# The forget-gate bias of eight attention heads: two matmuls against one-hot operands in place of one matmul against a prepared key tile

## The reference

```
log_f = jax.nn.log_sigmoid(f_logit + b_forget)          # 8 heads, 272 positions
cum = jnp.cumsum(log_f, axis=1).transpose(0, 2, 1)
s = (jnp.einsum('bhqd,bhkd->bhqk', q, k_f) * f_scale
     + c_q - cum[:, :, None, :])                        # c_q is cum at the query
p = jax.nn.softmax(jnp.where(mask, s, -jnp.inf), axis=-1)
o = jnp.einsum('bhqk,bhkd->bhqd', p, v_f)
```

## Time and profile before

| | |
|---|---|
| three runs | 2033.62, 2035.77 (the median), 2036.28 us |
| the profiled execution | 2033.62 us, of which the profile's span is 2031.8 us |
| PE busy | 1917.5 us, 94% of the span |
| DVE, ACT, POOL busy | 70%, 58%, 7% |
| matmul records | 10360, of them 96 of line 508 |

### The profile page before, as it was taken

The page is one execution under the profiler, slowest core; times in us unless marked ns, Lnnn a source line. Parts: engine busy times, 40 slices in busy tenths (PEclk is TensorE's granted clock), DMA queues, the critical chain, the costliest instruction groups (busy, mean ns, idle before and its releaser), DMA issues.

```text
span 2031.8 us, 28523 instructions
## 1 busy us (share of the span) xinstructions
PE 1917.5 (94%) x10360; PEld 1616.7 (80%) x10360; DVE 1432.1 (70%) x1529; ACT 1185.5 (58%) x1298; POOL 141.2 (7%) x184
## 2 busy tenths in 40 slices
PE   6999989999879999878999999999999999999997
PEld 5986789757868999867887887878878788788785
DVE  5542545435885555785887888888888788887885
ACT  4443453434634444634777667676776767767774
POOL 0102101120520000330000000000000000000000
PEclk9985799758888999987999999999999999999998
DMA  6420244103334546332798988989989899898892
GB/s 262 156 73 1 101 148 143 42 1 132 124 128 154 188 141 208 104 105 104 300 349 323 351 340 326 358 318 347 352 330 343 318 353 355 321 342 336 344 348 82
DMA packets 67847, 464.84 MB, mean 229 GB/s; under 512 B 7990, under 2 KB 8662, under 8 KB 15926
## 3 DMA queue, kind: packets, MB, share of 16 engines
q1 hardware_dynamic: 67061, 461.15, 60.7%
q0 software_dynamic: 704, 2.63, 0.4%
HBM read 462.71 MB, written 1.05 MB: 228 GB/s over the span
## 4 chain that ended last, share of the span: by engine, by line
PE 82%; DVE 8%; issue 7%; ACT 2%; DMA 0%; POOL 0%; ACTq 0%; SPq 0%; DVEq 0%; POOLq 0%
PE bank L356 22%; PE bank L357 22%; PE bank L358 22%; DVE wlo L347 2%; PE bank L506 2%; PE bank L793 2%; PE bank L801 2%; PE bank L443 2%; DVE cacc L1369 2%; DVE csq L1369 1%; PE bank L546 1%; PE bank L547 1%; PE bank L830 1%; PE bank L508 1%; ACT whi L342 1%
## 5 line engine op out<-in xcount | busy, mean ns | idle before, releaser
L347 DVE TENSOR_TENSOR wlo<-raw,whi 128x2048 fp32r<-128x2048 f32 (+2 forms) x454 | 1012.5, 2235 | 318.8 <-ACT whi L342 317.8
L342 ACT ACTIVATE whi<-raw 128x2048 fp32r<-128x2048 f32 (+2 forms) x454 | 844.7, 1863 | 278.9 <-PE bank L358 276.7
L356 PE MATMUL bank<-uhi,whi 128*128 128x272 f32 (+2 forms) x1200 | 355.2, 296 | 27.9 <-DVE ulo L1191 20.2
L356 PE MATMUL bank<-whi,hthi 128*128 128x512 f32 x896 | 366.9, 410 | 7.8 <-DVE wlo L347 7.8
L357 PE MATMUL bank<-wlo,hthi 128*128 128x512 f32 x896 | 356.2, 398 | 0.0
L358 PE MATMUL bank<-whi,htlo 128*128 128x512 f32 x896 | 356.0, 397 | 0.0
L358 PE MATMUL bank<-uhi,wlo 128*128 128x272 f32 (+2 forms) x1200 | 348.7, 291 | 0.0
L357 PE MATMUL bank<-ulo,whi 128*128 128x272 f32 (+2 forms) x1200 | 348.4, 290 | 0.0
L356 PEld LDWEIGHTS bank<-uhi,whi 128*128 128x128 f32 (+1 forms) x1200 | 232.0, 193 | 32.3 <-issue 22.8
L357 PEld LDWEIGHTS bank<-ulo,whi 128*128 128x128 f32 (+1 forms) x1200 | 232.0, 193 | 0.6
L358 PEld LDWEIGHTS bank<-uhi,wlo 128*128 128x128 f32 (+1 forms) x1200 | 231.6, 193 | 0.0
(11 more groups left out here) (276 smaller groups left out, 2256.1 us busy)
## 6 DMA issues: line engine op xcount, KB each, us to landing
raw<-in_wm SPq DMA_DIRECT2D x338, 1024.0 KB, 4.9
raw<-in_w SPq DMA_DIRECT2D x65, 1024.0 KB, 4.8
raw<-in_w SPq DMA_DIRECT2D x20, 768.0 KB, 4.1
raw<-in_w SPq DMA_DIRECT2D x16, 704.0 KB, 3.9
raw<-in_w SPq DMA_DIRECT2D x13, 512.0 KB, 3.6
raw<-in_w SPq DMA_DIRECT2D x2, 576.0 KB, 3.6
qk<-in_hT SPq DMA_DIRECT2D x1, 1088.0 KB, 9.1
gmb<-in_gmb POOLq DMA_DIRECT2D x1, 1024.0 KB, 6.7
```

What stands on the lines that cost most here:

```text
L342: act.activation(whi[:, n % RING, 0:c], raw[:, n % RAW, 0:c], ACT.Copy).then_inc(hi_ready, 1)
L347: dve.tensor_tensor(wlo[:, n % RING, 0:c], raw[:, n % RAW, 0:c], whi[:, n % RING, 0:c].bitcast(F32), ALU.subtract).then_inc(lo_ready, 1)
L356: pe.matmul(out, s_hi, m_hi, start=start, stop=False, skip_group_check=shared)
```

## The change

The 40-row matmul is replaced by two of 8 rows. The first has `ncum` as the stationary operand and, as the moving one, a one-hot column of the identity matrix, repeated over the keys with a step of zero. The second has the same column, repeated over the queries, as the stationary operand and `cum` as the moving one. `kcum`, `key_cum` and the semaphore `kcum_ready` go; PE waits for `cum_ready` instead. The copies go too, so that the logit tiles have 8 rows in place of 104, all at rows 0 to 7.

```diff
-FOX_AT = 32
-FOX_K = FOX_AT + FOX_HEADS
-FOX_ROWS = HEAD + FOX_K
-FOX_COPIES = (0, FOX_AT, HEAD, HEAD + FOX_AT)
...
-        cum = sb("cum", [FOX_ROWS, LEN], scope=first)
-        ncum = sb("ncum", [FOX_ROWS, LEN], scope=first)
-        kcum = sb("kcum", [FOX_ROWS, 2, LEN], scope=first)
+        cum = sb("cum", [FOX_HEADS, LEN], scope=first)
+        ncum = sb("ncum", [FOX_HEADS, LEN], scope=first)
...
-                    pe.wait_ge(kcum_ready, l * FOX_HEADS + (f + 1))
+                    pe.wait_ge(cum_ready, 2 * l + 2)
...
                     mm = pe.matmul(out, qk[part:part + HEAD, tq, q0:q0 + rows], qk[part:part + HEAD, tk, 0:keys], start=True, stop=not fox)
                     if fox:
-                        mm = pe.matmul(out, ncum[HEAD * (f % 2):HEAD * (f % 2) + FOX_K, q0:q0 + rows],
-                                       kcum[HEAD * (f % 2):HEAD * (f % 2) + FOX_K, (f // 2) % 2, 0:keys], start=False, stop=True)
+
+                        head = ident[0:FOX_HEADS, f:f + 1]
+                        pe.matmul(out, ncum[:, q0:q0 + rows], head.to_broadcast([FOX_HEADS, keys]), start=False, stop=False)
+                        mm = pe.matmul(out, head.to_broadcast([FOX_HEADS, rows]), cum[:, 0:keys], start=False, stop=True)
...
-            for at in (FOX_AT, HEAD + FOX_AT):
-                dve.memset(ncum[at:at + FOX_HEADS, :], 1.0)
...
-                    for at in (0, HEAD):
-                        op = dve.tensor_scalar(ncum[at:at + FOX_AT, :], cum[at:at + FOX_AT, :], -1.0, None, ALU.mult)
-                    op.then_inc(cum_ready, 1)
-                    for f in range(4):
-                        key_cum(l, f)
+                    dve.tensor_scalar(ncum[:], cum[:], -1.0, None, ALU.mult).then_inc(cum_ready, 1)
...
-                if 2 * DIFF_HEADS <= m < MAPS - 4:
-                    key_cum(l, m - 2 * DIFF_HEADS + 4)
```

More of the change, by code:

```diff
@@ L191, in build_program @@
         mask = sb("mask", [P, LEN], scope=first)
-        bforget = sb("bforget", [FOX_ROWS, LAYERS], scope=first)
+        bforget = sb("bforget", [FOX_HEADS, LAYERS], scope=first)
         subln = sb("subln", [P, LAYERS, DIFF_HEADS], scope=first)
@@ L200, in build_program @@
         h_in = qk[:, 0:KD, :]
-        xb, ab, lf = (ex[0:FOX_ROWS, i, 0:LEN] for i in range(3))
-        le, ll = sm[0:FOX_ROWS, 0, 0:LEN], sm[0:FOX_ROWS, 1, 0:LEN]
+        xb, ab, lf = (ex[0:FOX_HEADS, i, 0:LEN] for i in range(3))
+        le, ll = sm[0:FOX_HEADS, 0, 0:LEN], sm[0:FOX_HEADS, 1, 0:LEN]
         osb = qk[:, 4:8, :]
@@ L290, in build_program @@
         logit_step, lf_ready, cum_ready = sem("logit_step"), sem("lf_ready"), sem("cum_ready")
-        kcum_ready = sem("kcum_ready")
         s_done, masked, exp_done = sem("s_done"), sem("masked"), sem("exp_done")
@@ L923, in take_tile @@
                     act.wait_ge(par_landed, 16 * N_PAR)
-                    act.activation(xb, bank[i % 4][0:FOX_ROWS, 0:LEN], ACT.Identity,
+                    act.activation(xb, bank[i % 4][0:FOX_HEADS, 0:LEN], ACT.Identity,
                                    bias=bforget[:, bass.ds(l, 1)]).then_inc(proj_taken, 1)
@@ L931, in take_tile @@
                     act.wait_ge(logit_step, 3 * l + 2)
-                    act.activation(ll, le, ACT.Ln, bias=one[0:FOX_ROWS, :]).then_inc(logit_step, 1)
+                    act.activation(ll, le, ACT.Ln, bias=one[0:FOX_HEADS, :]).then_inc(logit_step, 1)
                 elif i < QK_T + ROPED:
@@ L1218, in _ @@
                 dve.tensor_copy(hT[:, k, :], h_in[:, k, :]).then_inc(x_ready, 1)
[L1221 to L1228, removed]
             def turned(l, i):
@@ L1235, in turned @@
                     dve.wait_ge(lf_ready, l + 1)
-                    dve.tensor_tensor_scan(cum[:], one[0:FOX_ROWS, :].to_broadcast([FOX_ROWS, LEN]), lf, 0.0,
+                    dve.tensor_tensor_scan(cum[:], one[0:FOX_HEADS, :].to_broadcast([FOX_HEADS, LEN]), lf, 0.0,
                                            ALU.mult, ALU.add).then_inc(cum_ready, 1)
                     dve.wait_ge(cum_ready, 2 * l + 1)
-                    for at in (0, HEAD):
-                        op = dve.tensor_scalar(ncum[at:at + FOX_AT, :], cum[at:at + FOX_AT, :], -1.0, None, ALU.mult)
-                    op.then_inc(cum_ready, 1)
-                    for f in range(4):
-                        key_cum(l, f)
+                    dve.tensor_scalar(ncum[:], cum[:], -1.0, None, ALU.mult).then_inc(cum_ready, 1)
                 elif QK_T <= i < QK_T + ROPED:
@@ L1720, in lay_out @@
         w_in = np.pad(a["w_in"][l], ((0, 0), (0, fl + P - a["w_in"].shape[2])))
-        for at in FOX_COPIES:
-            w_in[:, fl + at:fl + at + FOX_HEADS] = a["w_in"][l][:, fl:fl + FOX_HEADS]
         i = 0
@@ L1786, in lay_out @@
     io["ident"] = np.eye(P, dtype=f32)
[L1787 to L1790, removed]
+    io["bforget"] = a["b_forget"].T
     io["subln"] = per_feature(a["subln_g"])
```

## The result

The changed kernel takes 2070.8 us (median of four runs, 2070.6 to 2072.0) against 2035.5 us before, measured on the same chip: a ratio of 1.018, with an interval of 1.017 to 1.019. The forecast was 2073.5 us, from 2056 to 2081. It is slower, by 35.3 us where the sum had 38.7.

What follows compares the result with a forecast made beforehand. PE alone was taken to bound the fox maps, at 1.2 GHz: 1.45 + 0.87 + 0.10 = 2.42 us per map, 38.7 us over 16. With 2033.6 us profiled and 1.1 us for the median: 2073.5 us, range 2056 to 2081.

Steps and rivals of the forecast that it cites:

- the sum: Whole kernel: 38.7 us added to the profiled 2033.6 us, plus 1.1 us for a median, giving 2073.5 us.
- PE sets the pace of the fox maps: In all 16 fox maps of the attentions, PE work added or removed goes into the time one for one.
- The added matmul: Fox maps: nine matmuls replace six, the third of each tile costing 1.45 us per map in all.
- The added switches: Fox maps: changes of used array size between 8-row and 64-row matmuls cost 0.87 + 0.10 us per map.
- The choice of 8 rows as nearer to 16 than to 40: Fox maps: 8 rows beside 64 taken as a full switch, as 16 rows are, 0.16 + 0.13 us.
- The repeated operand: New matmuls' operand read with step zero: costs nothing; as a rival, 23 us more, 2096 us, chance 0.05.
- Nothing from DVE: Logit tile and fox maps: removing DVE's work gains 0, as PE has no listed wait there; otherwise some 8 us.
- The clock: Return to full clock after both attentions may shift: -3.4 to +3.4 us over both layers, taken as 0.
- the rival that it would rise: Fox maps: added work closes up PE's stream and the chip grants 2.4 GHz; 1984 us, chance 0.03.
- the rival of overlap: Odd fox maps: new matmuls run beside line 500 on other array rows; only 19.4 us added, 2054 us, chance 0.05.
- the rival without switches: Fox maps: 8 rows count as one size with 64, leaving only the matmuls, 23.2 us; 2057.9 us, chance 0.08.

Runs made afterwards that it cites:

- the kernel with 40 rows: Against the changed kernel, the one-hot bias matmuls have 40 rows at the head's own rows instead of 8 at row 0; 2054.6 us.
- order alone: The changed kernel's nine matmuls per fox map reordered, the three 64-row ones first, then the six 8-row ones; 2062.5 us, ratio 1.014 to the kernel before.
- The three kernels that part the switches from the rest: Against the changed kernel: 40 rows for 8 (2054.6 us); the query's 8-row bias matmul left out (2046.7 us); 64-row matmuls grouped first (2062.5 us).
- A step up by 3.65 us: The kernel before with each of DVE's makings of `kcum` done three times; 2044.6 us, ratio 1.005.
- the one without the query term: The changed kernel without the first of its two 8-row matmuls per tile, the query's bias; 2046.7 us, ratio 1.006 to the kernel before.
- the one with the bias in the mask: Bias matmuls leave PE; DVE adds the running sums, reloaded to 128 partitions, to the mask, query's bias left out; 2007.7 us against 2034.4 before.
- all eight kernels: The kernel before, the changed one and the six follow-up kernels; medians from 2007.7 us (bias in the mask) to 2070.8 us (changed).

## Why the prediction was right, step by step

*PE sets the pace of the fox maps:* right. Added work of 38.7 us was followed by 38.8 us in the attention (112.39 us in the first layer and 112.37 in the second), work of 23 us taken away by 23.0. (The 50.6 us of DVE in the earlier trace rows have "issue" for their releaser, which is no engine; that they are waits for the scores is borne out by the kernel and the starts, as said under the result, and not by that row.)

*The added matmul,* 1.45 us a map: right, 1.44 in the kernel with 40 rows.

*The added switches,* 0.97 us a map: right, 0.98, shown apart from the matmul, and once more by order alone. (The price of entering is 0.15 us at line 547, where the prediction has 0.16; line 506 gives 0.16.) The choice of 8 rows as nearer to 16 than to 40 held. The Trainium skill, TensorEngine Tiling (Array Packing), Key Properties, says that a change of the tiling mode drains the engine. The three kernels that part the switches from the rest agree with it, in that a cost stands where the size changes; the price, 0.13 us on leaving and 0.16 on entering at 1.2 GHz, is read from their starts.

*The repeated operand,* nothing: right, as line 510 against line 508 shows.

*Nothing from DVE:* right in size, wrong in its reason. PE was said to have no wait at the logit tile; it had one of 0.29 us, and no slack at all behind it. The step down was worth these gaps, 0.6 us in all. A step up by 3.65 us was paid whole, and with the clock's share on top. Luck had a part: the list was read as slack, and only the sign of the change kept that from costing anything. The list of waits couldn't show this, the distances between starts did.

*The clock,* taken as 0 with 3.4 us either way: the returns after the attentions took 6.2 us of half clock for 6.8 before, worth 0.3 us. The clock among the fox maps stayed at 0.50 in every kernel; the rival that it would rise is out. Odd and even maps are alike; the rival of overlap is out. No map takes 4.7 us with 8 rows; the rival without switches is out.

*The sum:* the profiled execution of the changed kernel spans 39.4 us more than that of before, 38.8 us in the attention and 0.6 us outside it (1846.4 for 1845.8 us), the sum's 38.7 nearly to the point. The median moved by 35.3. The 4.1 us between 39.4 and 35.3 lie in which executions were profiled: that of before took 1.9 us less than its median, and that of the changed kernel, 2073.0 us by its span and the 1.8 us around it, 2.2 us more. Against the sum 3.4 us are missing, and they are not explained. They are no work saved on DVE (0.6 us). The forecast added 1.1 us for a median where before has 1.9, and so ended 2.7 us above the result. Runs of one kernel spread over 1.4 to 5.5 us. In the 40-row kernel and in the one without the query term the times too stay 3.0 and 3.7 us under the attention's growth; in the one with the bias in the mask the gain is 3.7 us over it. Single profiles put the total of half clock outside the attention between 119 and 135 us, which moves the time by some 8 us from end to end. The 119 us are those of the kernel with the bias in the mask, 5.5 us of time less than the 130 of before, which is more than its 3.7. The profiles of before and of the changed kernel have 130 and 129 us, so that the clock doesn't part these two; that it parts the executions that weren't profiled is possible and not shown.

## What to carry to other kernels

When PE is without a gap, read the distances between starts, and price a small matmul by its columns and by its neighbours: a matmul over few rows is not cheap, and where its size differs from that of the matmul beside it (here 8 rows beside 64, but not 40 beside 64), it pays again on each side, 0.29 us together for 0.91 us of work at 1.2 GHz. Here padding 8 rows to 40 cost nothing; grouping matmuls of one size helps; best is to give a bias to an engine that waits. And no wait in the list doesn't mean slack: relieving an engine there may be worth nothing and burdening it may cost everything.

## What the runs showed that was not expected

A delay of 3.65 us on DVE at the logit tile cost 10 us of the kernel's time in two layers: the delay itself in each, and 1.7 and 2.8 us for the clock, which was at 0.50 for 3.4 and 5.7 us behind the wait. That is 11.8 us; some 0.6 us came back since the clock returned 1.9 us after the first attention and not 3.2. The profile is 10.9 us longer than that of before, the median 10.0. And PE's clock stays at 0.50 through 58 to 90 us of unbroken small float32 matmuls and transposes (58 us with the bias in the mask, 70 before, 89.5 in the changed kernel); it rose 1.6 to 4.6 us after the dense matmuls of the next stage had begun, over all eight kernels.
